# Seven-product tiles in the input projections of both blocks, and another order of the steps in the second block's mixers

## What is computed

```python
h = rms_norm(x, norm_gain[layer])
proj = h @ w_in[layer]                      # 1024 x 9304
(q_a, k_a, v_a, z_a, q_i, k_i, w_i, qkv_b, z_b, beta_l, a_l, gate_l) = split(proj)
y_a = dsa_attention(q_a, k_a, v_a, q_i, k_i, w_i) * silu(z_a)
qkv_b = silu(causal_depthwise_conv(qkv_b, conv_w[layer]))   # 3072 of the columns, 4 taps
q_b, k_b, v_b = split(qkv_b)                # q_b, k_b normalized
o_b = chunked_gated_delta_rule(q_b, k_b, v_b, beta, g)
y_b = rms_norm(o_b, gain) * silu(z_b)
x = x + (gates[0] * y_a + gates[1] * y_b) @ w_out[layer]
```

```python
u = rms_norm(h, norm_attn[i]) @ w_in[i]     # 1024 x 3228
o_a = nsa_attention(...); o_b = diff_attention(...)
o_c = gla_mixer(...);     o_d = hgrn2_mixer(...)
h = h + concat([o_a, o_b, o_c, o_d]) @ w_out[i]
c = rms_norm(h, norm_ffn[i])
h = h + (swiglu(c, ...) if i % 2 == 0 else moe_swiglu(c, ...))   # width 3584; top 2 of 8 experts
h = h + (p[i] @ ple_w_proj[i]) * sigmoid(rms_norm(h, ple_norm[i]) @ ple_w_gate[i])
```

## Time and profile before

| | us |
|---|---|
| median of 3 runs | 2407.88 |
| lowest and highest | 2404.06, 2408.59 |
| the profiled execution: time | 2409.21 |
| the profiled execution: span of the core | 2407.4 |
| mean granted TensorE clock | 0.990 |

### The profile page before, as it was taken

How to read it: one execution, slowest core, us unless ns; L and a number is a source line. 1 busy time by engine, 2 the same in 40 slices (tenths; PEclk the granted TensorE clock), 3 DMA queues, 4 the chain that set the end, 5 groups by cost and what they waited for, 6 DMA issues and landing times. The chain is left out here.

```text
span 2407.4 us, 51252 instructions
## 1 busy us (share of the span) xinstructions
PE 2354.6 (98%) x23229; PEld 1364.4 (57%) x23229; DVE 821.1 (34%) x1665; ACT 462.9 (19%) x794; POOL 139.7 (6%) x356
## 2 busy tenths in 40 slices
PE   9999999999999999999999899999999999999999
PEld 8755557855555676997455654435343534343444
DVE  3545623444543554666635531101010101101012
ACT  1532321432323542000025431000000000000001
POOL 5011000011000310000003100000000000000000
PEclk9999999999999999999999999999999999999999
DMA  7522334432335513445446128999999999999992
GB/s 246 168 89 72 122 123 140 137 108 79 104 100 148 176 55 120 154 169 183 158 133 187 52 93 342 397 402 378 405 397 409 379 387 399 369 384 396 388 369 97
DMA packets 194447, 542.56 MB, mean 225 GB/s; under 512 B 29200, under 2 KB 61360, under 8 KB 194224
## 3 DMA queue, kind: packets, MB, share of 16 engines
q1 hardware_dynamic: 180576, 536.82, 60.8%
q10 hardware_dynamic: 13344, 1.35, 0.5%
q0 software_dynamic: 304, 1.05, 0.1%
HBM read 538.12 MB, written 1.05 MB: 224 GB/s over the span
## 5 line engine op out<-in xcount | busy, mean ns | idle before, releaser
L407 PE MATMUL psum<-ring,hT 128*128 128x512 f32 (+3 forms) x1120 | 478.4, 576 | 6.0 <-ACT area L831 4.5
L2968 PE MATMUL psum<-ring,mix 128*32 128x448 f32 x4608 | 438.5, 539 | 0.7 <-DVE mix L3232 0.7
L407 PEld LDWEIGHTS psum<-ring,hT 128*128 128x128 f32 x1120 | 206.0, 190 | 206.4 <-issue 180.9
L2968 PEld LDWEIGHTS psum<-ring,mix 128*32 128x32 f32 x4608 | 148.8, 110 | 282.9 <-issue 280.7
L3221 DVE TENSOR_TENSOR area<-area,psum 128x1344 f32<-128x1344 f32 x16 | 24.6, 1535 | 470.6 <-PE psum L2968 470.6
L712 PE MATMUL psum<-hT,ring 128*128 128x256 f32 x768 | 166.4, 379 | 0.0
L712 PEld LDWEIGHTS psum<-hT,ring 128*128 128x128 f32 x768 | 145.9, 190 | 20.7 <-issue 1.0
L2981 PE MATMUL psum<-area 128*32 128x256 f32 x2688 | 148.2, 379 | 1.9 <-DVE area L3223 1.9
L2968 PE MATMUL psum<-area,mix 128*32 128x448 f32 x1536 | 147.2, 539 | 0.0
L2981 PE MATMUL psum<-ring,area 128*32 128x256 f32 x2688 | 146.5, 379 | 0.0
L2981 PEld LDWEIGHTS psum<-area 128*32 128x32 f32 x2688 | 86.5, 110 | 61.4 <-DVE area L3223 3.2
(11 more groups left out here) (592 smaller groups left out, 2581.5 us busy)
## 6 DMA issues: line engine op xcount, KB each, us to landing
ring<-in_w_in_dram SPq DMA_DIRECT2D x88, 1024.0 KB, 5.1
ring<-in_moe_w_gate_dram SPq DMA_DIRECT2D x96, 896.0 KB, 7.0
ring<-in_moe_w_up_dram SPq DMA_DIRECT2D x96, 896.0 KB, 8.0
area<-in_moe_w_down_dram SPq DMA_DIRECT2D x112, 512.0 KB, 5.9
ring<-in_moe_w_down_dram SPq DMA_DIRECT2D x112, 512.0 KB, 6.5
area<-in_moe_w_gate_dram SPq DMA_DIRECT2D x32, 896.0 KB, 7.3
area<-in_moe_w_up_dram SPq DMA_DIRECT2D x32, 896.0 KB, 7.6
ring<-in_w_out_dram SPq DMA_DIRECT2D x16, 1024.0 KB, 5.0
```

Of the source, the lines that this page charges most:

```text
L407: last = nc.tensor.matmul(acc(g)[:, t, 0:d["n"]], lhs(kk, t), w[:, k, :], start=kk == 0, stop=kk == d["nk"] - 1)
L2968: last = nc.tensor.matmul(PS[32 * j:32 * j + 32, 3 * p + b, 0:PIECE].rearrange("p (m n) -> p m n", n=32), tokens(k, b), w[:, :, j, :], sta ...
```

## The change

It has these parts.

1. **`qkv` tiles 1, 3 and 5** of each layer of the first block become seven-product tiles. TensorE issues 56 matmuls of 128 columns in place of 32 of 256. VectorE gets four token sums a layer, four weight sums and seven joins a tile. ScalarE's copy of such a tile (L771) is gone, and a copy of the first product stands in its place (`qkv_keep`). The first column sum moves from behind tile 3 into tile 4.
2. **`u` tiles 1 and 2** of each layer of the second block become seven-product tiles: 28 matmuls of 256 columns in place of 16 of 512. VectorE gets four token sums a layer, four weight sums and eight joins a tile.
3. **The plans** of the mixers are other strings. The zeroing of three buffers in `cmp_window` moves from VectorE to GpSimd.
4. **Table loads.** `table_of` issues a one-column ScalarE instruction with SiLU ahead of the wait for two `p1` tiles, and with Exp ahead of the wait for the maximum in sparse attention.
5. **Down projection.** The sums rotate through three places instead of two.
6. **Experts.** In the up part, the last four pieces run in another order.
7. **Start.** VectorE squares its half of x ahead of the parameter copy. Some setup semaphores are merged into others.

```diff
+        QKV_SEVEN = (1, 3, 5)
+        U_SEVEN = (1, 2)
...
+        def qkv_sums(s, L, i):
+            gs = group("qkv", L)
+            if i > 1:
+                s.eng.wait_ge(sem("weights_used"), used(TILES[gs[i - 2]]["first"]))
+            for h in range(2):
+                landed(s.eng, TILES[gs[i]]["first"] + h)
...
+            s.do(nc.vector.tensor_tensor(s1, lo[:, :, IN1], hi[:, :, IN1], ALU.add))
...
+        def qkv_seven(pe, L, i):
...
+            product(a, lo[:, :, IN0], HT[:, 0:4, TOK0]).then_inc(sem("seven_product"), 1)
+            pe.wait_ge(sem("seven_by_vector"), qkv_summed(L, i))
+            if i == 5:
+                pe.wait_ge(sem("gemm_out_act"), evacuated(gs[4])[1])
+            product(b, s2, t2).then_inc(sem("seven_product"), 1)
+            product(c, s1, t1).then_inc(sem("seven_product"), 1)
+            product(e, s3, t3).then_inc(sem("seven_product"), 1)
+            pe.wait_ge(sem("seven_kept"), qkv_kept(L, i))
+            product(a, hi[:, :, IN0], HT[:, 4:8, TOK0]).then_inc(sem("seven_product"), 1)
+            pe.wait_ge(sem("seven_by_vector"), qkv_read(L, i, 1))
+            product(b, s4, HT[:, 4:8, TOK1]).then_inc(sem("weights_used"), 1)
...
-                if i == 3:
-                    sums(0)
+                    if (i, j) == (4, 1):
+                        pe.wait_ge(sem("gemm_out_dve"), evacuated(group("qkv", L)[3])[1])
+                        sums(0)
+            pe.wait_ge(sem("seven_by_vector"), qkv_read(L, 5, 5))
...
+            qkv_token_sums(s)
+            qkv_sums(s, L, 1)
...
+                if j in QKV_SEVEN:
+                    qkv_quarters(s, L, j)
...
+                if j in (1, 3):
+                    qkv_sums(s, L, j + 2)
...
+                    if name == "p1" and max(a, Z0) < min(b, QI0):
+                        table_of(s, ACT.Silu)
...
+            table_of(s, ACT.Exp)
...
+        def u_seven(pe, L, i):
...
+            product(a, HT[:, 0:4, UTIMES[0]], lo[:, :, left]).then_inc(sem("seven_product"), 1)
...
         def u_dve(s, L):
+            u_token_sums(s)
+            u_weight_sums(s, L, 1)
+            if L == 0:
+                for t in range(T):
+                    s.after(nc.vector.tensor_scalar(X[:, t, :], XGAIN[:, t, :], RSTD1[:, t:t + 1], None, ALU.mult)
+                            .then_inc(sem("x_updated"), 1), "x_updated")
+            u_weight_sums(s, L, 2)
+            first, second = u_joins(s, L, 1), u_joins(s, L, 2)
+            next(first)
+            next(first)
             s.eng.wait_ge(sem("gla_z"), L + 1)
...
-        TENSOR_PLAN = "cfggffcgffdcnfnfcgfaffcggcfacffgffcfafcafdafffgffdgagfaaafafaaaggafaaafffffgffaafaaffaafffgfffffagaffgfg"
+        TENSOR_PLAN = "cfgfdnfcgffffgcfnggaffccgcfcfaffgdcffacfaaffaffgdfgaffgaafaafgaagafafffffgfaaafafffaafaffgffffafagagfffg"
...
-            s.do(nc.vector.memset(CX, 0.0))
+            s.eng.wait_ge(sem("cmp_cleared"), L + 1)
...
-            return 2 if i == 13 else i % 2
+            return i % 3
...
+            if q == 1:
+                order[-4:] = [(KD - 2, 0), (KD - 1, 0), (KD - 2, 1), (KD - 1, 1)]
```

More of the change, by code:

```diff
@@ L255, in span @@
         def span(group, w, c0, c1, evac, nk=KD):
-            for c in range(c0, c1, 512):
-                tile(group, w, c, min(512, c1 - c), evac, nk)
+            for i, c in enumerate(range(c0, c1, 512)):
+                tile(group, w, c, min(512, c1 - c), "dve" if group[0] == "qkv" and i in QKV_SEVEN else evac, nk)
         def pair(group, w, evac):
@@ new lines, in qkv_seven, with product @@
+        def qkv_seven(pe, L, i):
+            gs = group("qkv", L)
+            g = gs[i]
+            d = TILES[g]
+            lo, hi = quarter_operands(g)
+            s1, s2, s3, s4 = QSUM
+            t1, t2, t3, t4 = QTOK
+            a, b, c, e = qkv_parts(i)
+            def product(out, w, h):
+                for j in range(2):
+                    for k in range(4):
+                        last = nc.tensor.matmul(out[:, j, :], w[:, k, j * P:(j + 1) * P], h[:, k, :], start=k == 0, stop=k == 3)
+                return last
+            if i > 1:
+                name, value = evacuated(gs[i - 2])
+                pe.wait_ge(sem(name), value)
+            for h in range(2):
+                landed(pe, d["first"] + h)
+            product(a, lo[:, :, IN0], HT[:, 0:4, TOK0]).then_inc(sem("seven_product"), 1)
[9 more added lines that the diff above has]
+            product(b, s4, HT[:, 4:8, TOK1]).then_inc(sem("weights_used"), 1)
+            pe.wait_ge(sem("seven_by_vector"), qkv_read(L, i, 2))
+            product(c, hi[:, :, IN1], t4).then_inc(sem("weights_used"), 1)
@@ new lines, in u_weight_sums @@
+        def u_weight_sums(s, L, i):
+            g = group("u", L)[i]
+            for h in range(2):
+                landed(s.eng, TILES[g]["first"] + h)
+            lo, hi = u_weights(g)
+            t1, t2, t3, t4 = u_sums_of(i)
+            left, right = slice(0, 256), slice(256, 512)
+            add = nc.vector.tensor_tensor
+            s.do(add(t1, lo[:, :, right], lo[:, :, left], ALU.subtract))
+            s.do(add(t2, hi[:, :, right], t1, ALU.subtract))
+            s.do(add(t3, hi[:, :, right], lo[:, :, right], ALU.subtract))
+            s.after(add(t4, hi[:, :, left], t2, ALU.subtract).then_inc(sem("seven_by_vector"), 1), "seven_by_vector")
@@ new lines, in u_joins, with join @@
+        def u_joins(s, L, i):
+            g = group("u", L)[i]
+            a, b, c, e = u_parts(i)
+            x11, x12, x21, x22 = [u_quarter(g, t, half) for t in range(2) for half in range(2)]
+            def join(out, part, t, onto):
+                return nc.vector.scalar_tensor_tensor(out, part, RSTD[:, t:t + 1], onto, ALU.mult, ALU.add)
+            s.eng.wait_ge(sem("seven_kept"), 6 + 2 * L + i)
+            s.eng.wait_ge(sem("seven_product"), u_product(L, i, 2))
+            s.after(join(x11, b, 0, x12).then_inc(sem("u_read"), 1), "u_read")
+            s.eng.wait_ge(sem("seven_product"), u_product(L, i, 3))
+            s.do(join(x12, c, 0, x12))
+            s.after(join(x21, c, 1, x21).then_inc(sem("u_read"), 1), "u_read")
+            yield
+            s.eng.wait_ge(sem("seven_product"), u_product(L, i, 4))
+            s.do(join(x21, e, 1, x21))
+            yield
+            s.eng.wait_ge(sem("seven_product"), u_product(L, i, 5))
+            s.do(join(x22, a, 1, x21))
+            s.do(join(x12, a, 0, x12))
+            s.eng.wait_ge(sem("weights_used"), used(TILES[g]["first"]))
+            s.do(join(x21, b, 1, x21))
+            s.eng.wait_ge(sem("weights_used"), used(TILES[g]["end"] - 1))
+            s.after(join(x12, c, 0, x12).then_inc(sem("gemm_out_dve"), 1), "gemm_out_dve")
+            yield
@@ L1670, in u_dve @@
             gaps(s, nc.vector, 0, "gla_gaps")
+            next(second)
             s.eng.wait_ge(signal("hg_sig"), reached("hg_sig", L + 1))
```

266 lines of the change are left out of this document (198 added, 68 removed).

## The result

The changed kernel takes 2383.4 us (median of 4 runs, 2380.8 to 2386.3), before it was 2407.4: a ratio of 0.989 with an interval of 0.988 to 0.991. The forecast was 2381, 2364 to 2393. The profiled execution has a span of 2384.0 us, 23.4 less than before.

What follows compares the result with a forecast made beforehand. TensorE's work was taken to set the time, its waits second. Savings of 7.9 + 5.6 + 3.7 + 2.2 + 1.9 + 5.5 = 26.8 us took the profiled 2409.2 to 2382.4, the median to 2381; range 2364 to 2393.

Steps and rivals of the forecast that it cites:

- Term 1: `qkv` projection: three seven-product tiles a layer take 12.50 us each instead of 13.82, saving 7.9 us.
- room of 0.9 for the join: `qkv` tiles: VectorE's first join ends after 8.0 us, while five products take 8.9, leaving 0.9 us.
- Term 2: `u` tiles: seven-product tiles save 6.9 us, less a 1.3 wait for late VectorE in the first layer: 5.6 us.
- Term 3: SiLU and Exp table loads, issued ahead of the waits at `p1` tiles and in sparse attention, save 3.7 us.
- 2 × 1.28 = 2.6 go: `p1` tiles: loading SiLU's table ahead of the wait, once a layer, saves 1.28 us each, 2.6 in all.
- Terms 4 and 5: Down projection: a third place for sums removes a 2.2 us wait; experts: reordered pieces remove 1.9 of waiting for transposes.
- Term 6: Mixers: new plans shorten or cover TensorE's waits and recover some clock, saving 5.5 us between bounds of nothing and 16.
- 2.5 of the clock: Mixers: of the 13.0 us that the lower granted clock costs over both layers, 2.5 come back.
- rival B: Mixers: the new plans only move the waits, so the time is 2387 us, between 2384 and 2394; chance 0.22.
- C: Clock stays up through both mixers, the other 10.5 us come back: 2370 us, between 2360 and 2375; chance 0.23.
- D: VectorE is late in the seven-product tiles, the sixth products wait, 13.5 us are given back: 2395 us; chance 0.07.
- E: Slower: spread waits keep the mixers' clock mostly at its lower level, losing 69 us instead of 13: 2437; chance 0.03.

Runs made afterwards that it cites:

- x_by_scalar: The changed kernel with the two updates of x on ScalarE, ahead of its copies of u tile 0, instead of on VectorE: 2380.8 us, ratio 0.989.
- half_fill: The changed kernel with each mixer fill step multiplying only the first 128 of its 256 columns, a timing-only kernel: 2392.7 us, ratio 0.994.

## Why the prediction was right, and where it was not

**Term 1, `qkv` tiles: right.** 7.9 counted, 7.87 measured, 7.84 given back when they are undone. The room of 0.9 for the join was 0.8. What I had not seen is a new wait of 1.2 ahead of the first layer's decays (for L1043), gone with plain tiles.

**Term 2, `u` tiles: right in mechanism, too large.** 5.6 counted, 4.3 measured. The wait for VectorE behind the updates of x is there and is theirs (`x_by_scalar`), and a second one of 0.3 with it. The pace of a product is the 1.73 that I used, but a tile between transposes took 12.2 to 12.6 where I had 12.1.

**Term 3, table loads: right in the waits, mis-sized as a term.** 3.7 counted; 3.6 by the waits that return when it is undone. The step that left something out is "2 × 1.28 = 2.6 go": it prices the two waits and nothing behind them, and in the profile of before the clock had fallen behind both, 1.7 each. Beyond that the second layer's 5.5 holds the pause inside a run of TensorE's matmuls, which was not in my sum.

**Terms 4 and 5: mis-sized.** The step was to count the wait and nothing behind it: 2.2 and 1.9 against 4.1 and 4.1 measured. Of the first, 1.7 is the clock that had fallen behind the wait; in the experts 1.6 is the second row of waits, for VectorE's L3221, which goes by the same reordering.

**Term 6, mixers: wrong.** The step that failed is the gain itself, 1.1 a layer for the earlier copy, 0.8 for a wait put behind fill steps, and 2.5 of the clock. I followed one link of the chain, which did get shorter (2.1 to 1.2), and took for gain what only changed place: idle time before was 9.0 and 11.9 us, and with the new plans it is 11.7 and 11.5. The 2.5 of the clock is no fixed gain either: the loss to the clock in the mixers is 15 us in one profile of the changed kernel and 5 in the other, against 13 before. This is rival B's mechanism, inside a total that the other terms brought back to the forecast; that the rest gave 6.9 more than its 21.3 is luck. Without this term I had 21.3; the stages outside the mixers and the output gave 28.2 in the first profile, and those two took 4.8 back.

**The rivals.** C had the clock whole in both mixers: one profile of the changed kernel nearly shows it (0.98 and 0.97), another does not (0.94 and 0.92), so it is no property of the change. D did not happen: no join gated a `qkv` tile. E's lever is real, though not from this change: in `half_fill` the clock's loss was 47 us.

No version beats the changed kernel clearly. The one with the updates of x on ScalarE has the lowest median, 2380.8, and a shorter stage for it, within the interval of the changed kernel.

## What to carry to other kernels

Price a wait of TensorE by what follows it too: behind the waits of 1.8 to 2.2 us here the granted clock fell five times of nine and behind the four pauses of 1.9 to 2.9 each time, and a fall cost some 1.7, about as much again. For a stage with many short waits compare idle time (length less busy time) between profiles, not its length, and take a second profile of the same kernel before believing a difference of 3 us. When a step is moved ahead, list what each engine waits for around its new place, the evacuation of the shared accumulators as well as the one wait that it is to remove.

## What was not expected of the hardware

The same program's mixers took 104.5 and 109.9 us in two profiles with the same idle time, by the granted clock alone. Less work for TensorE made the kernel slower by 9 us. A run of 64 equal matmuls stopped after the 56th for 1.9 to 2.9 us in the three kernels with plain `qkv` tiles and in none with seven-product tiles, each time with a packet of the instruction queue landing about then, behind a weight load; that one caused the other is not shown.
